# Rotary embedding without rotation products: ScalarE exchanges 32-row blocks of q and k

## The chip, the core and the metric

The program runs on one core of a Trainium2 chip. The core has four compute engines that run their own instruction streams and meet by semaphores: TensorE (matrix products into PSUM, in the profile PE, its weight loads PEld), VectorE (DVE), ScalarE (ACT) and GpSimd (POOL). SyncE (SP) issues most DMAs. The metric is the device time of one execution in microseconds, the median of several runs.

## What is computed

A transformer block of one kind (dilated attention, a rwkv recurrence, gates, a feed-forward part) is followed by one of another kind (three attention branches, memory attention, a feed-forward part), on 256 tokens of width 1024. The change touches the rotary embedding of q and k, which both blocks have in the same form:

```python
def rope(x, pos):
    half = HEAD_DIM // 2                                   # 32
    inv_freq = ROPE_THETA ** (-jnp.arange(0, HEAD_DIM, 2, dtype=jnp.float32) / HEAD_DIM)
    ang = pos[:, None] * inv_freq[None, :]
    ...
    c, s = jnp.cos(ang), jnp.sin(ang)
    x1, x2 = xf[..., :half], xf[..., half:]
    return jnp.concatenate([x1 * c - x2 * s, x2 * c + x1 * s], axis=-1).astype(x.dtype)
```

With features on partitions, a head has 64 rows. Each row needs itself times the cosine and the row 32 away, in the same head, times the sine with a sign.

## The kernel before

Everything is fp32. A large product is made of three products in a rounded format: ScalarE copies a weight tile to its rounded part (L1827, `parts<-low`), VectorE subtracts that from the tile (L2710), and TensorE multiplies both parts (L807, L808 and L816 in a chunk of features; L721 to L723 in a token range). The tile is split in two halves, 4 of its 8 rows of 128 features each in a chunk; TensorE waits for each half before its first use. Two buffers hold rounded parts, so tile j + 1 is split while TensorE works on tile j, and only after tile j - 1 is done.

Every engine's program is written out in the same order: generators for the main work and for side work are stepped by `Turns`, and each engine executes its own stream strictly in order. A moved or added instruction therefore delays all that stands behind it on its engine.

**Block one** (the profile's 92 to 152 us): `qkv()` has six chunks of q and k with 256 features and 256 tokens each (`feature_chunk`, streams of 24 products for each half of the features), and between their steps the chain of the rwkv part (`chain()`), one level a chunk, levels 1 to 5. In a level TensorE makes the T products (L1192, L1195) right at the end of a chunk, VectorE masks them out of PSUM in four instructions of 64 rows (L3002: two for the first half of the tokens, then two for the second), and TensorE makes the X products (L1217 to L1225, the first and then the second half), which wait for the masks of their half. A chunk n of q or k goes through these hands: ScalarE copies the bank to `rz1` (L1827, `mid<-psum`), VectorE multiplies the bank by the cosine (L2816), which frees the bank, TensorE multiplies `rz1` by a signed permutation into another bank (L766, at the sixth product pair of chunk n + 1), VectorE multiplies that by the sine (L2783) and adds (L2822). On VectorE the order in a chunk's turn is: cosine, masks of the level, masks of another rwkv product, sine, sum, the two split halves.

**Block two** (502 to 529 us): `main_b()` has four chunks (n = 2 to 5) of 256 features, one (n = 6) of 128, and then a token range of 464 columns. ScalarE copies the bank to `rz2`, which frees the bank; POOL multiplies by the cosine (L3701), TensorE makes the rotation (L766) inside chunk n + 1, VectorE multiplies it by the sine (L2783) from PSUM into `RC`, and POOL adds (L3706). On VectorE the order in a chunk's turn is: sine of the chunk before, then the two split halves for the next chunk. On ScalarE it is: read of the chunk that ended, then the two halves.

Of the kernel before, what the change touches and what calls it, by code (L numbers as in the profile page):

```python
# [11 lines left out]
ALU = mybir.AluOpType  # L12
# [7 lines left out]
S0 = math.exp(-0.5)  # L20


C_ID, C_SU, C_IU, C_LI, C_ONE, C_BLK, C_ROT, C_M0, C_D64 = [128 * i for i in range(9)]
C_LV = 128 * 9
C_MA = C_LV + 768
C_CA = C_MA + 768
C_ST = C_CA + 256
# [17 lines left out]
def shape_constants():  # L45
    c = np.zeros((128, C_END), np.float32)
    i = np.arange(128)
    r, s = i[:, None], i[None, :]
    c[:, C_ID:C_ID + 128] = r == s
    c[:, C_SU:C_SU + 128] = r < s  # L50
    c[:, C_IU:C_IU + 128] = r <= s
    c[:, C_LI:C_LI + 128] = r >= s
    c[:, C_ONE:C_ONE + 128] = 1
    c[:, C_BLK:C_BLK + 128] = r // 64 == s // 64
    same = r // 64 == s // 64
    c[:, C_ROT:C_ROT + 128] = (same & (r % 64 < 32) & (s % 64 == r % 64 + 32)) * 1.0 \
        - (same & (r % 64 >= 32) & (s % 64 == r % 64 - 32)) * 1.0
    for n in range(7):
        b = 1 << n
        m = (r // (2 * b) == s // (2 * b)) & (r // b % 2 == 1) & (s // b % 2 == 0)  # L60
        if n == 0:
            c[:, C_M0:C_M0 + 64] = (r % 2 == 1) & (s[:, 0:64] == r % 64 - 1)
            c[:, C_M0 + 64:C_M0 + 128] = ((r % 2 == 0) & (s[:, 0:64] == r % 64 + 1)) | (s[:, 0:64] == r % 64)
        else:
            c[:, C_LV + 128 * (n - 1):C_LV + 128 * n] = m | (r == s)
    c[:, C_D64:C_D64 + 64] = r % 64 < s[:, 0:64]
    c[:, C_D64 + 64:C_D64 + 128] = r % 64 == s[:, 0:64]
    for n, keep in enumerate([s >= r, s <= r, (r - s) % 4 == 0, ((r - s) % 4 == 0) & (s <= r),
                              (r - s) % 16 == 0, ((r - s) % 16 == 0) & (s <= r)]):
# [12 lines left out]
    c[:, C_COS:C_COS + 256] = np.tile(cos, (4, 1))  # L82
    c[:, C_SIN:C_SIN + 256] = np.tile(sin, (4, 1))
    c[0:64, C_COSC:C_COSC + 256] = np.tile(cos, (2, 1))
    c[64:128, C_COSC:C_COSC + 256] = 1
    c[0:64, C_SINC:C_SINC + 256] = np.tile(sin, (2, 1))
    return c


# [187 lines left out]
def program(nc, A, consts, vecs, pt, out):  # L277
    with ExitStack() as ctx:
# [55 lines left out]
        def const(off, n):  # L334
            return low[:, OC + off:OC + off + n]
# [234 lines left out]
        z_act, z_dve, z_pool = count("z_act"), count("z_dve"), count("z_pool")  # L570
        split_act, split_dve = count("split_act"), count("split_dve")
        main_pe, main_act, main_dve, main_pool = [count("main_" + n) for n in ("pe", "act", "dve", "pool")]
        rope_pe, rope_act, rope_dve, rope_pool = [count("rope_" + n) for n in ("pe", "act", "dve", "pool")]
        rw_pe, rw_act, rw_dve, rw_pool = [count("rwkv_" + n) for n in ("pe", "act", "dve", "pool")]
        at_pe, at_act, at_dve = [count("attn_" + n) for n in ("pe", "act", "dve")]
        up_pe, up_act, up_dve = [count("up_" + n) for n in ("pe", "act", "dve")]
# [131 lines left out]
        def tensor_program(e, turns):  # L708
# [42 lines left out]
            def seam(tag, i, at_once=False):  # L751
                yield
                if at_once:
                    for _ in turn(tag, i, XN):
                        pass
                    yield
                    yield
                else:
                    yield from turn(tag, i, XN)

            def rotate(tag, n, m, z):

                b = 2 + n % 2 if tag == "qk" else 5 + n % 3
                p = bank(b)
                q.wait_ge(*rope_act.at(tag, n))
                mm(p[:, 0:256 * m], const(C_ROT, 128), z, True, True).then_inc(rope_pe.up(tag, n), 1)  # L766
                free[b] = [rope_dve.at(tag, n)]

            def head(tag, banks, freed, late):

# [227 lines left out]
            def qkv():  # L998
                for s in range(3, 7):
                    yield from feature_chunk(st1, s, next(pg), plan_z[s][1], z_read(s), nothing)  # L1000
                yield from token_range(st1, V_AT, 2, 512, lambda i: [main_act.at("v", 0, i)], nothing)
                yield from token_range(st1, V_AT + 2, 1, 256, lambda i: [main_act.at("v", 1, i)], nothing)
                for n in range(6):
                    yield from feature_chunk(st1, QK_AT + n, next(pg), [128, 128], [rope_dve.at("qk", n, "cos")],
                                             (lambda n=n: rotate("qk", n - 1, 2, rz1[(n - 1) % 2])) if n else nothing)

            def gate(r, late):
                yield from token_range(st1, GATE_AT[r], 2, 512, lambda i: [main_act.at("g1", r, i)], late)

            def gates():  # L1010
                for r in (2, 3, 0, 1):
                    yield from gate(r, (lambda: rotate("qk", 5, 2, rz1[1])) if r == 2 else nothing)

            rw_bank = itertools.cycle((4, 5, 6, 7))

# [440 lines left out]

            st2 = ST["st2"]

            def rotate2(n):
                if n >= 2:  # L1460
                    m = 1 if n == 6 else 2
                    rotate("in2", n, m, rz2[n % 2][:, 0:m, :])

            def read2(n):
                return [main_act.at("qa", n) if n < 2 else rope_act.at("in2", n)]

            turns.beside(head("in2", (0, 2), read2, lambda n: rotate2(n - 1)), seam("in2", 1, True), 3)

            def main_b():
                for n in range(2, 7):  # L1470
                    yield from feature_chunk(st2, n - 2, next(pg), plan_2[n][1], read2(n), lambda n=n: rotate2(n - 1))
                yield from token_range(st2, 5, 2, 464, lambda i: [main_act.at("vt2", i), main_dve.at("vt2", i)], lambda: rotate2(6))

            turns.alone(main_b())

# [338 lines left out]
        def scalar_program(e, turns):  # L1814
# [3 lines left out]
            def bank(b):  # L1818
                return PSUM[:, b, :]
# [6 lines left out]
            def copy(o, a):  # L1826
                return e.activation(o, a, ACT.Copy)  # L1827
# [158 lines left out]
                turns.alone(feature_chunk(st1, s, plan_z[s][1], lambda: z_read(s, b)))  # L1986


            def rope_read(tag, n, m, b, zs):
                if n >= (2 if tag == "qk" else 4):  # L1990
                    q.wait_ge(*(rope_pe.at(tag, n - 2) if tag == "qk" else rope_pool.at(tag, n - 2)))
                copy(zs, halves(bank(b))[:, 0:m, :]).then_inc(rope_act.up(tag, n), 1)

            def qkv():
                for s in range(3, 7):
# [625 lines left out]
        def vector_program(e, turns):  # L2621
# [3 lines left out]
            def bank(b):  # L2625
                return PSUM[:, b, :]
# [151 lines left out]
                tt(rview(P + 11776 + 256 * k, 256), hid[:, k, :], rview(base + 1024, 256).bitcast(F32), ALU.subtract) \  # L2778
                    .then_inc(down_dve.up(tag, "al", k), 1)

            def rotate(tag, n, m, dst, sin):
                q.wait_ge(*rope_pe.at(tag, n))
                tt(dst, halves(bank(2 + n % 2 if tag == "qk" else 5 + n % 3))[:, 0:m, :], rep(sin, m), ALU.mult).then_inc(rope_dve.up(tag, n), 1)  # L2783


            for i in range(2):
# [30 lines left out]

            def rotate1(n):
                dst = qk[:, 2 * n:2 * n + 2, :]
                rotate("qk", n, 2, dst, const(C_SIN, 256))  # L2820
                q.wait_ge(*rope_dve.at("qk", n))
                tt(dst, dst, rt1[n % 2], ALU.add).then_inc(rope_dve.up("qk", n, "sum"), 1)  # L2822

# [472 lines left out]

            def rotate2(n):
                if n >= 2:
                    rotate("in2", n, 1 if n == 6 else 2, rope_to(n), const(C_SINC if n == 6 else C_SIN, 256))

            turns.beside(head("in2", st2, nothing, lambda n: rotate2(n - 1)), seam_ple(1), 3)

# [358 lines left out]
        def gpsimd_program(e, turns):  # L3661
# [35 lines left out]
                            yield  # L3697

            def rope(tag, n, m, zs, t1, cos):
                q.wait_ge(*rope_act.at(tag, n))  # L3700
                tt(t1, zs, rep(cos, m), ALU.mult).then_inc(rope_pool.up(tag, n, "cos"), 1)  # L3701

            def rotate(tag, n, dst, t1):
# [36 lines left out]
            def gate(r, late):  # L3740
                yield from token_range(st1, GATE_AT[r], 2, late)
# [246 lines left out]
```

## Time and profile before

| what | us |
|---|---|
| runs | 911.99, 912.70, 912.81 (median 912.7) |
| the profiled execution | 912.49, its span 910.7 |
| TensorE busy | 890.3 |
| VectorE busy | 604.7 |
| ScalarE busy | 454.3 |
| GpSimd busy | 44.3 |

The granted clock of TensorE is 0.998 of full speed over the span. Busy time of TensorE includes overlaps of neighbouring products, so starts of instructions tell more than their durations. A row of a timeline shows an instruction's start and duration; what stands in brackets is the time its engine was idle before it, and who ended that.

### The profile page before, as it was taken

How to read it: one execution, taken by the hardware profiler on the slowest of the kernel's cores; microseconds unless marked ns; L12 is line 12 of the kernel's file. 1: busy time of each engine (PE TensorE's matmuls, PEld its weight loads, DVE VectorE, ACT ScalarE, POOL GpSimd, SP SyncE). 2: the span in 40 equal slices, each digit the busy share in tenths (PEclk: the TensorE clock that was granted, in tenths of full speed). 3: DMA queues.
4: the chain of work that ended last, by engine and by line, in shares of the span. 5: the costliest groups of instructions: out<-in, count | busy, mean ns of one | idle time of the engine just before them, and what ended most of it. 6: DMA issues, size and time to landing. Idle time of an engine off the chain costs nothing.

```text
span 910.7 us, 15439 instructions
## 1 busy us (share of the span) xinstructions
PE 890.3 (98%) x6574; PEld 752.5 (83%) x6574; DVE 604.7 (66%) x966; ACT 454.3 (50%) x731; POOL 44.3 (5%) x61
## 2 busy tenths in 40 slices
PE   7999999999899999999999999999999999999997
PEld 5999988787789888888889978776788788888885
DVE  4577978557766666656766477877863566666673
ACT  4775444346443444546544356484622545555561
POOL 0010000010000000000000440000000000000000
PEclk9999999999999999999999999999999999999999
DMA  9544333233578665555339574353817566665521
GB/s 341 186 139 140 97 100 110 72 95 117 206 254 278 185 185 187 189 202 203 108 130 222 137 223 145 127 186 96 276 44 208 141 188 189 192 192 192 200 95 47
DMA packets 131205, 150.78 MB, mean 166 GB/s; under 512 B 11808, under 2 KB 102176, under 8 KB 131008
## 3 DMA queue, kind: packets, MB, share of 16 engines
q1 hardware_dynamic: 129920, 145.57, 51.6%
q10 hardware_dynamic: 1216, 4.23, 1.2%
q8 instruction: 52, 0.85, 0.4%
q14 instruction: 17, 0.14, 0.0%
HBM read 148.73 MB, written 1.05 MB: 164 GB/s over the span
## 4 chain that ended last, share of the span: by engine, by line
PE 90%; DVE 4%; ACT 2%; issue 2%; DMA 1%; POOL 0%; POOLq 0%; ACTq 0%; DVEq 0%
PE psum L834 12%; PE psum L721 10%; PE psum L723 9%; PE psum L722 9%; PE psum L839 7%; PE psum L807 4%; PE psum L808 4%; PE psum L816 4%; PE psum L787 4%; PE psum L727 3%; PE psum L883 2%; PE psum L893 2%; PE psum L884 2%; PE psum L840 2%; PE psum L1724 2%
## 5 line engine op out<-in xcount | busy, mean ns | idle before, releaser
L1827 ACT ACTIVATE parts<-low 128x1024 fp32r<-128x1024 f32 (+3 forms) x252 | 254.3, 1044 | 66.3 <-PE psum L723 50.2
L2710 DVE TENSOR_TENSOR parts<-low,parts 128x1024 fp32r<-128x1024 f32 (+3 forms) x156 | 187.9, 1234 | 27.6 <-ACT parts L1827 27.4
L721 PE MATMUL psum<-parts 128*128 128x512 f32 (+2 forms) x424 | 169.4, 399 | 1.8 <-DVE parts L2710 1.0
L723 PE MATMUL psum<-parts 128*128 128x512 f32 (+2 forms) x424 | 163.5, 386 | 0.0
L722 PE MATMUL psum<-parts 128*128 128x512 f32 (+2 forms) x424 | 163.4, 385 | 0.0
L1827 ACT ACTIVATE high<-psum 128x512 f32<-128x512 f32 (+4 forms) x95 | 52.4, 562 | 162.0 <-PE psum L840 76.4
L834 PE MATMUL psum<-parts 128*128 128x512 f32 x462 | 116.8, 392 | 0.0
L834 PEld LDWEIGHTS psum<-parts 128*128 128x128 f32 x462 | 86.9, 188 | 16.9
L721 PEld LDWEIGHTS psum<-parts 128*128 128x128 f32 x424 | 79.6, 188 | 23.3 <-issue 4.0
L723 PEld LDWEIGHTS psum<-parts 128*128 128x128 f32 x424 | 79.6, 188 | 16.3
L722 PEld LDWEIGHTS psum<-parts 128*128 128x128 f32 x424 | 79.8, 188 | 14.2 <-issue 0.2
L2775 DVE TENSOR_TENSOR parts<-low,parts 128x1024 fp32r<-128x1024 f32 x54 | 66.0, 1222 | 35.3 <-ACT parts L1827 35.3
L807 PE MATMUL psum<-parts 128*128 128x256 f32 (+2 forms) x312 | 82.3, 300 | 0.0
L808 PE MATMUL psum<-parts 128*128 128x256 f32 (+2 forms) x312 | 76.8, 282 | 0.0
L839 PEld LDWEIGHTS psum<-parts 128*128 128x128 f32 x528 | 72.0, 190 | 5.1
L839 PE MATMUL psum<-parts 128*128 128x256 f32 x528 | 73.6, 282 | 0.0
L807 PEld LDWEIGHTS psum<-parts 128*128 128x128 f32 (+2 forms) x312 | 58.9, 189 | 4.1 <-issue 3.2
L808 PEld LDWEIGHTS psum<-parts 128*128 128x128 f32 (+2 forms) x312 | 59.0, 189 | 2.3 <-issue 2.2
L3206 DVE TENSOR_TENSOR mid<-psum,high 128x512 f32<-128x512 f32 x33 | 22.8, 691 | 46.2 <-ACT high L1827 46.2
L816 PE MATMUL psum<-parts 128*128 128x256 f32 (+2 forms) x312 | 43.8, 283 | 0.0
L3669 POOL TENSOR_TENSOR low<-low 128x1 f32<-128x1 f32 x20 | 11.0, 550 | 632.3 <-DVE low L2634 316.2
L816 PEld LDWEIGHTS psum<-parts 128*128 128x128 f32 (+2 forms) x312 | 40.0, 189 | 0.1
(317 smaller groups left out, 1340.0 us busy)
## 6 DMA issues: line engine op xcount, KB each, us to landing
low<-in_w_in_dram SPq DMA_DIRECT2D x40, 1024.0 KB, 5.3
low<-in_w_ffn_in_dram SPq DMA_DIRECT2D x44, 512.0 KB, 5.2
low<-in_w_ff_in_dram SPq DMA_DIRECT2D x16, 1024.0 KB, 5.9
low<-in_w_ff_out_dram SPq DMA_DIRECT2D x16, 1024.0 KB, 4.9
low<-in_w_ffn_out_dram SPq DMA_DIRECT2D x11, 1024.0 KB, 4.9
low<-in_w_out_dram SPq DMA_DIRECT2D x8, 1024.0 KB, 5.3
low<-in_w_ple_gate_dram SPq DMA_DIRECT2D x4, 1024.0 KB, 4.9
low<-consts_dram ACTq DMA_DIRECT2D x1, 2142.0 KB, 9.0
```

Of the source, the lines that this page charges most:

```text
L721: mm(o, l[0], r[0], start, False)
L722: mm(o, l[0], r[1], False, False)
L723: return mm(o, l[1], r[0], False, stop)
L787: t = mm(PSUM[0:m, banks[n], 256 * j + 128 * i:256 * j + 128 * i + 128], w3[:, k, off:off + m], uT[:, k, 128 * i:128 * i + 128], k == 0, k ...
L807: mm(o, hi[:, k, c], st.uh[:, k, :], k == 0, False)
L808: mm(o, lo_[:, k, c], st.uh[:, k, :], False, False)
L816: t = mm(o, hi[:, k, c], st.ul[:, k, :], False, k == 7)
L834: mm(p, hi[:, k, c], st.u2(k), k == 0, False)
L839: mm(p[:, 0:256], lo_[:, k, c], st.uh[:, k, :], False, False)
L1827: return e.activation(o, a, ACT.Copy)
L2710: tt(rslot3(n, nk, width)[:, r, 0:w], slot3(n, nk, width)[:, r, 0:w], st.hi3(j)[:, r, 0:w].bitcast(F32), ALU.subtract) \
L2775: tt(rview(OR + 2048 * n + 1024 * (k % 2), 1024), slot(n)[:, 1024 * (k % 2):1024 * (k % 2) + 1024], rview(base, 1024).bitcast(F32), ALU.su ...
```

## The change

The permutation matrix `C_ROT` leaves the constants, and with it the eleven products L766 and their semaphore. The sine table carries the sign: minus in the first 32 rows of a head, plus in the others. ScalarE makes the exchange of 32-row blocks with four copies (`swapped`) out of the bank of the chunk.

- In block one these four copies take the place of the one copy to `rz1`; the cosine on VectorE still reads the bank and waits, as before, for ScalarE's read of it. The sine reads `rz1`.
- In block two the straight copy to `rz2` stays, for POOL's cosine, with a semaphore step of its own (`"z"`), and the four copies go straight to the place in `RC`; the sine then works in place there. The bank is free after the four copies.

```diff
-            def rotate(tag, n, m, z):
-
-                b = 2 + n % 2 if tag == "qk" else 5 + n % 3
-                p = bank(b)
-                q.wait_ge(*rope_act.at(tag, n))
-                mm(p[:, 0:256 * m], const(C_ROT, 128), z, True, True).then_inc(rope_pe.up(tag, n), 1)
-                free[b] = [rope_dve.at(tag, n)]
...
+            def swapped(dst, z):
+
+                for p in range(4):
+                    t = copy(dst[32 * p:32 * p + 32], z[32 * (p ^ 1):32 * (p ^ 1) + 32])
+                return t
+
             def rope_read(tag, n, m, b, zs):
-                if n >= (2 if tag == "qk" else 4):
-                    q.wait_ge(*(rope_pe.at(tag, n - 2) if tag == "qk" else rope_pool.at(tag, n - 2)))
-                copy(zs, halves(bank(b))[:, 0:m, :]).then_inc(rope_act.up(tag, n), 1)
+                z = halves(bank(b))[:, 0:m, :]
+                if tag == "qk":
+                    if n >= 2:
+                        q.wait_ge(*rope_dve.at(tag, n - 2))
+                    swapped(zs, z).then_inc(rope_act.up(tag, n), 1)
+                else:
+                    if n >= 4:
+                        q.wait_ge(*rope_pool.at(tag, n - 2, "cos"))
+                    copy(zs, z).then_inc(rope_act.up(tag, n, "z"), 1)
+                    swapped(rope_to(n), z).then_inc(rope_act.up(tag, n), 1)
...
-            def rotate(tag, n, m, dst, sin):
-                q.wait_ge(*rope_pe.at(tag, n))
-                tt(dst, halves(bank(2 + n % 2 if tag == "qk" else 5 + n % 3))[:, 0:m, :], rep(sin, m), ALU.mult).then_inc(rope_dve.up(tag, n), 1)
+            def rotate(tag, n, m, zs, dst, sin):
+                q.wait_ge(*rope_act.at(tag, n))
+                tt(dst, zs, rep(sin, m), ALU.mult).then_inc(rope_dve.up(tag, n), 1)
...
             def rope(tag, n, m, zs, t1, cos):
-                q.wait_ge(*rope_act.at(tag, n))
+                q.wait_ge(*rope_act.at(tag, n, "z"))
                 tt(t1, zs, rep(cos, m), ALU.mult).then_inc(rope_pool.up(tag, n, "cos"), 1)
```

On ScalarE in block two, from the third chunk's read to the copies that follow the half-sized chunk (`high<-psum` is the read of a chunk, `parts<-low` a split half), the order before is:

```order
L1827 ACTIVATE high<-psum 128x512
L1827 ACTIVATE parts<-low 128x4x128 x2
L1827 ACTIVATE high<-psum 128x512
L1827 ACTIVATE parts<-low 128x928 x2
L1827 ACTIVATE high<-psum 128x256
L1827 ACTIVATE high<-high 64x256 x3
```

and now, where L1810 is the same helper:

```order
L1810 ACTIVATE high<-psum 128x512
L1810 ACTIVATE high<-psum 32x512 x4
L1810 ACTIVATE parts<-low 128x4x128 x2
L1810 ACTIVATE high<-psum 128x512
L1810 ACTIVATE high<-psum 32x2x256 x4
L1810 ACTIVATE parts<-low 128x928 x2
L1810 ACTIVATE high<-psum 128x256
L1810 ACTIVATE high<-psum 32x256 x4
L1810 ACTIVATE high<-high 64x256 x3
```

Four copies have come between each read and the split halves that follow it.

On VectorE in block one, two turns with levels 1 and 2 of the chain (`mid<-psum,low` at L2816 is the cosine, L2783 the sine, L2822 the sum, L3002 the masks), the order before is:

```order
L2816 TENSOR_TENSOR mid<-psum,low 128x512
L3002 TENSOR_TENSOR high<-psum,low 64x512 x4
L2978 TENSOR_TENSOR high<-psum,low 128x4x128 x2
L2783 TENSOR_TENSOR mid<-psum,low 128x512
L2822 TENSOR_TENSOR mid<-mid 128x512
L2710 TENSOR_TENSOR parts<-low,parts 128x1024 x2
L2816 TENSOR_TENSOR mid<-psum,low 128x512
L3002 TENSOR_TENSOR high<-psum,low 64x512 x4
```

and now:

```order
L2812 TENSOR_TENSOR mid<-psum,low 128x512
L2998 TENSOR_TENSOR high<-psum,low 64x512 x4
L2974 TENSOR_TENSOR high<-psum,low 128x4x128 x2
L2779 TENSOR_TENSOR mid<-mid,low 128x512
L2818 TENSOR_TENSOR mid<-mid 128x512
L2706 TENSOR_TENSOR parts<-low,parts 128x1024 x2
L2812 TENSOR_TENSOR mid<-psum,low 128x512
L2998 TENSOR_TENSOR high<-psum,low 64x512 x4
```

Nothing has moved on VectorE; the sine alone has another source, SBUF in place of a bank.

## Rows read from the trace of the kernel before

**Rows 1.** The page: busy time by engine, and engines of the last chain.

```profile
PE 890.3 (98%) x6574; PEld 752.5 (83%) x6574; DVE 604.7 (66%) x966; ACT 454.3 (50%) x731; POOL 44.3 (5%) x61
...
PE 90%; DVE 4%; ACT 2%; issue 2%; DMA 1%; POOL 0%; POOLq 0%; ACTq 0%; DVEq 0%
```

**Rows 2.** View of line L766, block one: count, ns min/median/max, first and last start, shape.

```profile
L766 PE MATMUL psum<-mid,low x12: 590/590/594, 94.3 to 148.2; 128*128 128x512 f32 x12
```

**Rows 3.** Timeline of TensorE, a rotation of block two: start, us, engine, line, operation.

```profile
502.85 1.02 PE L766 MATMUL psum<-high,low 128*128 128x512 f32 x2
...
503.83 0.28 PE L808 MATMUL psum<-parts 128*128 128x256 f32 x1
```

**Rows 4.** Timeline of ScalarE, block two: reads of chunks, and two split halves.

```profile
495.86 0.60 ACT L1827 ACTIVATE high<-psum 128x512 f32<-128x512 f32 x1 [1.09 <-PE psum L787]
496.35 2.00 ACT L1827 ACTIVATE parts<-low 128x1024 fp32r<-128x1024 f32 x2
501.61 0.60 ACT L1827 ACTIVATE high<-psum 128x512 f32<-128x512 f32 x1 [3.26 <-PE psum L816]
...
521.43 0.60 ACT L1827 ACTIVATE high<-psum 128x512 f32<-128x512 f32 x1 [4.97 <-PE psum L816]
```

**Rows 5.** Timeline of VectorE, block two: a sine and the two split halves behind it.

```profile
503.91 0.69 DVE L2783 TENSOR_TENSOR high<-psum,low 128x512 f32<-128x512 f32 x1 [4.12 <-PE psum L766]
504.60 1.22 DVE L2710 TENSOR_TENSOR parts<-low,parts 128x1024 fp32r<-128x1024 f32 x1
...
505.75 2.31 DVE L2710 TENSOR_TENSOR parts<-low,parts 128x1024 fp32r<-128x1024 f32 x1
```

**Rows 6.** Timeline of GpSimd in the same stretch: a cosine and a sum.

```profile
502.29 1.28 POOL L3701 TENSOR_TENSOR high<-high,low 128x512 f32<-128x512 f32 x1 [15.90 <-ACT high L1827]
504.68 2.30 POOL L3706 TENSOR_TENSOR high<-high 128x512 f32<-128x512 f32 x1 [1.11 <-DVE high L2783]
```

**Rows 7.** Timeline of TensorE: the token range's first product, and its first after both waits.

```profile
525.51 0.47 PE L721 MATMUL psum<-parts 128*128 128x464 f32 x1 [0.39 <-DVE parts L2710]
...
527.63 0.48 PE L721 MATMUL psum<-parts 128*128 128x464 f32 x1 [0.17 <-DVE parts L2710]
```

**Rows 8.** Groups of ScalarE with shapes apart: a copy of 15 rows; busy us, mean ns.

```profile
L1827 ACT ACTIVATE high<-psum 15x512 f32<-15x512 f32 x1 | 0.6, 568 | 0.0
```

**Rows 9.** Timeline of ScalarE, block one: reads in levels 3 to 5; pairs of 64-row copies.

```profile
123.21 0.60 ACT L1827 ACTIVATE mid<-psum 128x512 f32<-128x512 f32 x1 [1.92 <-PE psum L816]
...
134.37 0.60 ACT L1827 ACTIVATE mid<-psum 128x512 f32<-128x512 f32 x1 [1.92 <-PE psum L816]
...
145.31 0.60 ACT L1827 ACTIVATE mid<-psum 128x512 f32<-128x512 f32 x1 [1.98 <-PE psum L816]
...
151.37 1.08 ACT L1827 ACTIVATE high<-psum 64x512 f32<-64x512 f32 x2 [3.57 <-PE psum L1221]
...
152.47 1.21 ACT L1827 ACTIVATE high<-psum 64x512 f32<-64x512 f32 x2
```

**Rows 10.** Timeline of VectorE, block one: start of its work, masks of level 1, level 3.

```profile
90.51 0.45 DVE L2964 COPY_PREDICATED high<-low,psum 128x256 f32<-128x256 int32 x1 [0.99 <-PE psum L1132]
...
103.47 2.84 DVE L3002 TENSOR_TENSOR high<-psum,low 64x512 f32<-64x512 f32 x4
...
123.83 0.69 DVE L2816 TENSOR_TENSOR mid<-psum,low 128x512 f32<-128x512 f32 x1 [2.80 <-ACT mid L1827]
124.44 2.84 DVE L3002 TENSOR_TENSOR high<-psum,low 64x512 f32<-64x512 f32 x4
```

**Rows 11.** Timeline of TensorE, block one: first X product of levels 1, 3, 4, 5.

```profile
106.55 0.27 PE L1217 MATMUL psum<-high 64*64 64x64 f32 x1
...
129.17 0.27 PE L1217 MATMUL psum<-high 64*64 64x64 f32 x1
...
139.73 0.27 PE L1217 MATMUL psum<-high 64*64 64x64 f32 x1
...
150.13 0.27 PE L1217 MATMUL psum<-high 64*64 64x64 f32 x1
```

More of the change, by code:

```diff
@@ L20 @@
 S0 = math.exp(-0.5)
-C_ID, C_SU, C_IU, C_LI, C_ONE, C_BLK, C_ROT, C_M0, C_D64 = [128 * i for i in range(9)]
-C_LV = 128 * 9
+C_ID, C_SU, C_IU, C_LI, C_ONE, C_BLK, C_M0, C_D64 = [128 * i for i in range(8)]
+C_LV = 128 * 8
 C_MA = C_LV + 768
@@ L54, in shape_constants @@
     c[:, C_BLK:C_BLK + 128] = r // 64 == s // 64
-    same = r // 64 == s // 64
-    c[:, C_ROT:C_ROT + 128] = (same & (r % 64 < 32) & (s % 64 == r % 64 + 32)) * 1.0 \
-        - (same & (r % 64 >= 32) & (s % 64 == r % 64 - 32)) * 1.0
     for n in range(7):
@@ L82, in shape_constants @@
     c[:, C_COS:C_COS + 256] = np.tile(cos, (4, 1))
-    c[:, C_SIN:C_SIN + 256] = np.tile(sin, (4, 1))
+    c[:, C_SIN:C_SIN + 256] = np.tile(np.concatenate([-sin, sin]), (2, 1))
     c[0:64, C_COSC:C_COSC + 256] = np.tile(cos, (2, 1))
     c[64:128, C_COSC:C_COSC + 256] = 1
-    c[0:64, C_SINC:C_SINC + 256] = np.tile(sin, (2, 1))
+    c[0:64, C_SINC:C_SINC + 256] = np.concatenate([-sin, sin])
     return c
@@ L572, in program @@
         main_pe, main_act, main_dve, main_pool = [count("main_" + n) for n in ("pe", "act", "dve", "pool")]
-        rope_pe, rope_act, rope_dve, rope_pool = [count("rope_" + n) for n in ("pe", "act", "dve", "pool")]
+        rope_act, rope_dve, rope_pool = [count("rope_" + n) for n in ("act", "dve", "pool")]
         rw_pe, rw_act, rw_dve, rw_pool = [count("rwkv_" + n) for n in ("pe", "act", "dve", "pool")]
@@ L1003, in qkv @@
                 for n in range(6):
-                    yield from feature_chunk(st1, QK_AT + n, next(pg), [128, 128], [rope_dve.at("qk", n, "cos")],
-                                             (lambda n=n: rotate("qk", n - 1, 2, rz1[(n - 1) % 2])) if n else nothing)
+                    yield from feature_chunk(st1, QK_AT + n, next(pg), [128, 128], [rope_dve.at("qk", n, "cos")], nothing)
             def gate(r, late):
@@ L1011, in gates @@
                 for r in (2, 3, 0, 1):
-                    yield from gate(r, (lambda: rotate("qk", 5, 2, rz1[1])) if r == 2 else nothing)
+                    yield from gate(r, nothing)
             rw_bank = itertools.cycle((4, 5, 6, 7))
@@ L1457, in tensor_program @@
             st2 = ST["st2"]
[L1459 to L1462, printed above, removed]
             def read2(n):
                 return [main_act.at("qa", n) if n < 2 else rope_act.at("in2", n)]
-            turns.beside(head("in2", (0, 2), read2, lambda n: rotate2(n - 1)), seam("in2", 1, True), 3)
+            turns.beside(head("in2", (0, 2), read2, nothing), seam("in2", 1, True), 3)
             def main_b():
                 for n in range(2, 7):
-                    yield from feature_chunk(st2, n - 2, next(pg), plan_2[n][1], read2(n), lambda n=n: rotate2(n - 1))
-                yield from token_range(st2, 5, 2, 464, lambda i: [main_act.at("vt2", i), main_dve.at("vt2", i)], lambda: rotate2(6))
+                    yield from feature_chunk(st2, n - 2, next(pg), plan_2[n][1], read2(n), nothing)
+                yield from token_range(st2, 5, 2, 464, lambda i: [main_act.at("vt2", i), main_dve.at("vt2", i)], nothing)
             turns.alone(main_b())
@@ L2819, in rotate1 @@
                 dst = qk[:, 2 * n:2 * n + 2, :]
-                rotate("qk", n, 2, dst, const(C_SIN, 256))
+                rotate("qk", n, 2, rz1[n % 2], dst, const(C_SIN, 256))
                 q.wait_ge(*rope_dve.at("qk", n))
@@ L3298, in rotate2 @@
                 if n >= 2:
-                    rotate("in2", n, 1 if n == 6 else 2, rope_to(n), const(C_SINC if n == 6 else C_SIN, 256))
+                    rotate("in2", n, 1 if n == 6 else 2, rope_to(n), rope_to(n), const(C_SINC if n == 6 else C_SIN, 256))
             turns.beside(head("in2", st2, nothing, lambda n: rotate2(n - 1)), seam_ple(1), 3)
```

## Prediction

> **What bounds the kernel now.** The page first: TensorE is busy 890.3 of 910.7 us, and 90% of the chain that ended last is TensorE's own work [rows 1]. So a product taken off TensorE is worth its whole time, as long as nobody whom TensorE waits for gets later. Then the view of the line that goes: its twelve records in block one are six products, since one fp32 product runs as two records [rows 2]. TensorE's timeline prices one: the rotation begins at 502.85 and the second chunk product behind it at 503.83, while chunk products follow each other every 0.12 us; 0.98 - 0.12 leaves 0.86 a rotation [rows 3]. ScalarE's reads, which begin as a chunk ends, say the same: 5.75 us for the chunk without a rotation (495.86 to 501.61), and 19.82 for the next three (to 521.43), 6.61 each [rows 4]. Ten rotations of 512 columns and one of 256: 10 x 0.86 + 0.43 = **9.0 us** leaves TensorE.
>
> **What is added.** ScalarE reads a q or k chunk with four copies of 32 rows (block one, in place of one copy), or with the straight copy and then four (block two). No row shows a 32-row copy. A copy of 15 rows and 512 columns takes 568 ns, about as long as one of 128 rows (0.60 in [rows 4]), so rows are not what is paid for [rows 8]. The open question is how densely they follow. Copies of 64 rows stand at a step of 0.49 where both read the same half of the partitions (1.08 for two) and of 0.61 where the half changes (1.21 for two) [rows 9]. The new copies change their rows each time, so I take **0.60**, with 0.49 as the lower end. ScalarE's read then takes 2.4 instead of 0.6 in block one, and 0.49 + 2.4 = 2.9 in block two. ScalarE is idle before these reads (3.26 and 4.97 us in [rows 4]), so its own time is covered; what costs is what stands behind the read on VectorE: in block one the cosine on the same bank and, behind it, the masks of the rwkv chain; in block two the sine and both halves of the weight split. The sine itself gets no dearer from SBUF: a split half with both inputs there takes 1.22 for 1024 columns, the sine from the bank 0.69 for 512 [rows 5]. The constants' transfer, 3% shorter, ends long before these places: nothing.
>
> **Block one, by levels of the chain.** Times count from s, the start of ScalarE's read. Before, the cosine begins at s + 0.62 (123.21, 123.83), the four masks L3002 at s + 1.23, the first pair ends at s + 2.65 and the second at s + 4.07 [rows 9, 10]. After, all of it is 1.8 later (2.4 for 0.6): pairs at 4.45 and 5.87, with 0.1 for the semaphore **4.55 and 5.97**. TensorE comes to the first half of the X products (L1217) at s + 5.96, 5.36 and 4.82 in levels 3, 4 and 5 (129.17, 139.73, 150.13) [rows 9, 11]; level 2 lies as level 3. Without the rotation that stands ahead of them it comes 0.86 sooner, and to the second half 1.0 later than to the first.
> - Level 1: two rotations are gone, and TensorE would come at 104.8 instead of 106.55. But VectorE has worked from 90.5 on, and its masks end at 104.9 and 106.31 [rows 10]; the second half begins at 106.4 instead of 107.5. Gain 1.1 of 1.7.
> - Levels 2 and 3: 5.10 against 4.55 needed, 6.10 against 5.97. No wait; gain 2 x 0.86.
> - Level 4: 4.50 and then 5.55, against 4.55 and 5.97: waits 0.45. Gain 0.4.
> - Level 5: 3.96 against 4.55, then 5.55 against 5.97: waits 1.0. Gain -0.1.
>
> Block one: 1.1 + 1.7 + 0.4 - 0.1 = **3.1 us** of 5.2. The splits of the next weights end 1.8 later too, but TensorE comes to them only after the next level's first products, over 1 us behind them.
>
> **Block two.** Here the splits decide. Before, POOL's sum starts right behind the sine, and then POOL and VectorE hinder each other: the sum takes 2.30 where the cosine of the same size takes 1.28, and a split half takes 2.31 where the one before it took 1.22 [rows 5, 6]. I read this as turns: VectorE's half (to 505.75), the sum (to 507.0), VectorE's other half (to 508.05). After: copies until s + 2.9, sine until 3.6, and now the sum is first, because ScalarE's half comes only at 3.85 (two halves take 2.00 [rows 4]); sum until 5.0, VectorE's halves done at **6.15 and 7.3**. TensorE, without its rotation, ends the chunk at 5.75 and wants the second half 0.96 (eight products) after the first: at the third chunk it waits 0.4 + 0.2. By that delay it finds the halves ready one chunk on, and the ones after have 512 columns. Three rotations less the wait: 3 x 0.86 - 0.6 = 2.0.
>
> The last place costs. Behind the fourth chunk (read at 521.43) stands a half-sized chunk of 2.9 us, and then the token range, whose weights can be split only after that read. Before, the range begins at 525.51, waiting for VectorE, and its second part at 527.63, which is 6.24 after the fourth chunk's end (0.04 before the read); between them lie six products, 2.12 less the rotation's 0.43 and the wait's 0.17, 1.5 [rows 4, 7]. After: copies 2.9, sine 3.6, sum 5.0, a half of 928 columns to 6.05; the range begins at s + 6.1 and its second part at s + 7.6. That is **1.4 later**, though two rotations stood here. Block two is worth 2.0 - 1.4 = **0.6**.
>
> The Trainium skill, page "SBUF — State Buffer", section "Who interferes with whom", says that a VectorE instruction with two SBUF inputs and a GpSimd one that reads SBUF exclude each other for a whole instruction; the sine gets its first input from SBUF now and would join them. By that rule, the rows on split and sum agree (2.31 against 1.22). It would speak against this change only where the sine meets POOL's cosine; that is over 2.0 after s (502.29 + 1.28 against 501.61 [rows 4, 6]) and the sine begins at s + 2.95, so the sum stays as it is.
>
> **Sum.** 3.1 + 0.6 = **3.7 us** saved. The profiled execution took 912.49 us (span 910.7 and 1.8 around it), the median of the runs is 912.7: **909.0**.
>
> **Rivals.**
> - *Dense copies.* At a step of 0.49 block one's read is done at 2.0, so that levels 4 and 5 wait 0.1 and 0.7 (3.8 saved); in block two the third chunk doesn't wait and the range's second part is 0.9 late: 2.6 - 0.9 = 1.7. Together 5.5, **907.2**. For it: pairs on the same rows show 0.49. Against: the pair that changes rows shows 0.61. Chance 0.20.
> - *All of it hidden.* 9.0 saved, **903.7**. Against: in level 1 VectorE is busy for 16 us before its masks, whatever TensorE does. 0.06.
> - *Absorbed later.* Behind 155 us gates, attention and rwkv share an order fixed in advance. If another engine bounds a stretch there, block one's gain is lost and block two's 0.6 is left: **912.1**, no change. For it: TensorE is idle for 20.4 us of the span. Against: 90% of the chain is TensorE, so most of what it waits for was released by itself and moves along. 0.14.
> - *Slower: the 32-row copies are dearer than every row here.* The same places: at a step of 0.9 the masks are 1.2 later still, the levels wait 0.4, 1.0, 1.0, 1.5 and 2.0, and block one loses 0.7; in block two the third chunk waits 1.8 and the range's second part is 2.5 late: 2.6 - 1.8 - 2.5 = -1.7. Together -2.4, **915.1**. It is no gain from a step of 0.78, and slower beyond doubt from 0.88. Against: copies of 15, 64 and 128 rows all take 0.57 to 0.61. 0.07.
>
> **How the numbers follow.** The forecast has 0.53. About 0.2%, 1.8 us, can be told from no change by a measurement of this kernel. Faster: forecast, dense and hidden, 0.79; same: 0.14; slower: 0.07. The range reaches from 905.8, below the dense copies, to 911.6; it leaves out all hidden, slower and half of absorbed.
>
> **What would show it.** In the profile after: eleven products fewer; 32-row copies of 0.59 at a step of 0.60; block one's cosine 2.4 behind ScalarE's read; new waits of TensorE for the masks in levels 1, 4 and 5, none in 2 and 3; in block two a short wait for the split at the third chunk and one of about 3 us before the token range, with POOL's sum back at 1.3 and ahead of the split. A step under 0.5 or over 0.7, or a range that begins without a long wait, would make the sum wrong; so would new idle time behind 155 us.

## The result and the profile after

| what | before | after |
|---|---|---|
| median of the runs, us | 912.81 (911.99 to 912.85, five runs) | 915.81 (915.40 to 917.31, five runs) |
| the profiled execution, us | 912.49, span 910.7 | 915.76, span 914.0 |
| TensorE busy, us | 890.3 | 884.0 |
| ScalarE busy, us | 454.3 | 476.8 |

The changed kernel takes 1.0041 times as long (95% interval 1.0029 to 1.0052): its median is **3.0 us higher**, where 3.7 us less was forecast, and lies above the range of 905.8 to 911.6.

The page of the kernel after, its busy times and the shares of the last chain, answers to [rows 1]:

```profile
PE 884.0 (97%) x6552; PEld 750.7 (82%) x6552; DVE 604.7 (66%) x966; ACT 476.8 (52%) x769; POOL 41.3 (5%) x61
...
PE 85%; DVE 8%; ACT 4%; issue 2%; DMA 1%; POOL 0%; POOLq 0%; ACTq 0%; DVEq 0%
```

The 22 records of the eleven rotations are gone. But VectorE and ScalarE, which had 6% of the chain, now have 12%: the chain leaves TensorE more often. The question is where.

**Block one.** The timeline of ScalarE after gives the reads of levels 2 to 5, now four copies in a row each (start, duration of the four, in brackets the idle time ahead):

```profile
111.97 2.38 ACT L1810 ACTIVATE mid<-psum 32x512 f32<-32x512 f32 x4 [1.98 <-PE psum L805]
123.56 2.39 ACT L1810 ACTIVATE mid<-psum 32x512 f32<-32x512 f32 x4 [1.98 <-PE psum L805]
135.15 2.39 ACT L1810 ACTIVATE mid<-psum 32x512 f32<-32x512 f32 x4 [1.98 <-PE psum L805]
147.25 2.38 ACT L1810 ACTIVATE mid<-psum 32x512 f32<-32x512 f32 x4 [1.98 <-PE psum L805]
```

Four copies take 2.39, a step of 0.60 as forecast. But from 123.56 to 135.15 it is 11.59, where it was 11.16 before [rows 9], although a rotation has gone from each chunk. TensorE's timeline after names who it waits for, at the first X product of each half in levels 3, 4 and 5, and of the first half in level 1 (L1205 was L1217; level 2 reads as level 3):

```profile
106.39 0.24 PE L1205 MATMUL psum<-high 64*64 64x64 f32 x1 [1.27 <-DVE high L2998]
...
129.57 0.24 PE L1205 MATMUL psum<-high 64*64 64x64 f32 x1 [0.82 <-DVE high L2998]
...
130.89 0.24 PE L1205 MATMUL psum<-mid,high 64*64 64x64 f32 x1 [0.16 <-DVE high L2981]
...
141.16 0.24 PE L1205 MATMUL psum<-high 64*64 64x64 f32 x1 [1.42 <-DVE high L2998]
...
142.98 0.24 PE L1205 MATMUL psum<-mid,high 64*64 64x64 f32 x1 [0.65 <-DVE mid L2988]
...
151.82 0.24 PE L1205 MATMUL psum<-high 64*64 64x64 f32 x1 [0.57 <-DVE high L2998]
...
153.26 0.24 PE L1205 MATMUL psum<-mid,high 64*64 64x64 f32 x1 [0.28 <-DVE high L2998]
```

And this is the view of waits from 85 to 160 us (us in total, times, the longest):

```profile
DVE mid L2812 <- ACT mid L1810: 12.8, 4, 3.2
...
PE psum L1205 <- DVE high L2998: 5.2, 6, 1.4
```

VectorE's cosine (L2812) waits for the read, and TensorE waits 5.2 us for the masks behind it (L2998), also in levels 2 and 3, for which no wait was forecast. In VectorE's timelines, the first of the custom instructions that follow the chain, of the kernel before and of the kernel after, shows that the place is left 2.20 us later:

```profile
154.70 0.56 DVE L3090 CUSTOM_DVE_ANT_1 mid<-psum,low 128x384 f32<-128x384 f32 x1 [1.60 <-PE psum L1346]
```

```profile
156.90 0.56 DVE L3086 CUSTOM_DVE_ANT_1 mid<-psum,low 128x384 f32<-128x384 f32 x1
```

**From there to block two** nothing changes. The first read of [rows 4] that a rotation follows, at 501.61, now stands at 503.84, 2.23 later.

**Block two.** ScalarE's timeline after has the reads 5.75, 6.74 and 5.76 apart, 18.25 for three chunks, where it was 19.82:

```profile
503.84 3.02 ACT L1810 ACTIVATE high<-psum 128x512 f32<-128x512 f32 x5 [3.26 <-PE psum L805]
...
509.59 3.01 ACT L1810 ACTIVATE high<-psum 128x512 f32<-128x512 f32 x5 [0.70 <-PE psum L805]
...
516.33 3.02 ACT L1810 ACTIVATE high<-psum 128x512 f32<-128x512 f32 x5 [1.69 <-PE psum L805]
...
522.09 3.02 ACT L1810 ACTIVATE high<-psum 128x512 f32<-128x512 f32 x5 [1.56 <-PE psum L805]
```

GpSimd's sum takes 1.29 and not 2.30 [rows 6], and VectorE's two split halves behind it end at 507.98 + 3.20 = 511.18, 7.34 behind the read:

```profile
507.66 1.29 POOL L3702 TENSOR_TENSOR high<-high 128x512 f32<-128x512 f32 x1 [1.86 <-DVE high L2779]
```

```profile
507.98 3.20 DVE L2706 TENSOR_TENSOR parts<-low,parts 128x1024 fp32r<-128x1024 f32 x2 [0.40 <-ACT parts L1810]
```

Then the token range, in TensorE's timeline after. It begins 6.22 behind the fourth read, after the only long wait of the stage, and the sixth product stands 0.38 behind the fifth where 0.21 is the usual step:

```profile
528.31 0.45 PE L718 MATMUL psum<-parts 128*128 128x464 f32 x1 [3.38 <-DVE parts L2706]
...
529.01 0.40 PE L718 MATMUL psum<-parts 128*128 128x464 f32 x1
529.22 0.58 PE L719 MATMUL psum<-parts 128*128 128x464 f32 x1
529.60 0.59 PE L720 MATMUL psum<-parts 128*128 128x464 f32 x1
```

The view by stretches of time says what that is. The columns are: the stretch, its length, busy time and count of PE, PEld, DVE, ACT and POOL, the granted clock of TensorE, the busy share of the DMA engines, GB/s:

```profile
524.80:528.20 3.40, 0.13 (x2) 0.00 (x0) 2.75 (x3) 3.30 (x7) 2.00 (x2) 1.00 1.02 225
528.20:529.20 1.00, 0.89 (x4) 0.86 (x5) 1.00 (x1) 0.96 (x3) 0.56 (x1) 1.00 1.00 381
529.20:532.40 3.20, 3.20 (x10) 2.59 (x10) 1.97 (x4) 2.86 (x5) 2.25 (x3) 0.50 1.03 403
532.40:536.00 3.60, 3.60 (x18) 3.22 (x17) 1.11 (x2) 0.75 (x1) 3.60 (x15) 0.97 0.14 56
```

A microsecond after the wait the granted clock is 0.50, the lower of its two levels (1.2 GHz), for 3.2 us. In the kernel before it is 1.00 at this place, with the DMA engines just as busy:

```profile
528.00:530.00 2.00, 2.00 (x11) 1.80 (x10) 1.03 (x1) 1.81 (x2) 1.86 (x4) 1.00 1.06 401
```

The two waits of [rows 7] had been 0.39 and 0.17.

As a marker of the end of this stage serves the read of twelve columns on ScalarE, at 534.53 before and 538.00 after. It has moved by 3.47 us, of which 2.23 came from block one; block two adds 1.24.

### The profile page after: what moved, and what is told of

Read it like the earlier page. It is cut to its first block, busy times and chain, and to the rows that moved or that the text cites. A ratio compares the mean times of both kernels' runs of the same rounds, so it can differ in the third digit from the quotient of the medians.

```text
span 914.0 us, 15434 instructions
## 1 busy us (share of the span) xinstructions
PE 884.0 (97%) x6552; PEld 750.7 (82%) x6552; DVE 604.7 (66%) x966; ACT 476.8 (52%) x769; POOL 41.3 (5%) x61
## 4 chain that ended last, share of the span: by engine, by line
PE 85%; DVE 8%; ACT 4%; issue 2%; DMA 1%; POOL 0%; POOLq 0%; ACTq 0%; DVEq 0%
PE psum L823 12%; PE psum L718 9%; PE psum L720 9%; PE psum L719 9%; PE psum L828 7%; PE psum L776 4%; PE psum L796 3%; PE psum L797 3%; PE psum L805 3%; PE psum L724 3%; PE psum L872 2%; PE psum L882 2%; PE psum L873 2%; PE psum L829 2%; PE psum L1707 2%
## 5 line engine op out<-in xcount | busy, mean ns | idle before, releaser
L1810 ACT ACTIVATE parts<-low 128x1024 fp32r<-128x1024 f32 (+3 forms) x252 | 254.3, 1044 | 66.4 <-PE psum L720 51.4
L1810 ACT ACTIVATE high<-psum 128x512 f32<-128x512 f32 (+6 forms) x115 | 63.3, 559 | 143.3 <-PE psum L829 76.4
L796 PE MATMUL psum<-parts 128*128 128x256 f32 (+2 forms) x312 | 79.1, 291 | 0.9 <-ACT high L1810 0.6
L797 PE MATMUL psum<-parts 128*128 128x256 f32 (+2 forms) x312 | 76.5, 283 | 0.0
L1810 ACT ACTIVATE mid<-psum 32x512 f32<-32x512 f32 (+7 forms) x55 | 29.2, 547 | 31.9 <-PE psum L805 13.5
L805 PE MATMUL psum<-parts 128*128 128x256 f32 (+2 forms) x312 | 43.8, 283 | 0.0
```

What stands on the lines that cost most here:

```text
L796: mm(o, hi[:, k, c], st.uh[:, k, :], k == 0, False)
L797: mm(o, lo_[:, k, c], st.uh[:, k, :], False, False)
L805: t = mm(o, hi[:, k, c], st.ul[:, k, :], False, k == 7)
```

## Experiments

A run's marks are read at three places: the read that ends a chunk at each level, the instruction with which block one is left (154.70 before, 156.90 after), and the twelve-column read (534.53 and 538.00). A is in each expectation the theory that is being put forward, B its rival.

**Where it is lost: each block alone.** The first kernel has the change in block one only, with block two's rotation restored:

```diff
-                    copy(zs, z).then_inc(rope_act.up(tag, n, "z"), 1)
-                    swapped(rope_to(n), z).then_inc(rope_act.up(tag, n), 1)
+                    copy(zs, z).then_inc(rope_act.up(tag, n), 1)
...
+                    yield from feature_chunk(st2, n - 2, next(pg), plan_2[n][1], read2(n), lambda n=n: rotate2(n - 1))
```

> Block one alone as in the changed kernel, block two with its rotation products and single copies as before. Theory A (the first half of a level's X products waits for all four masks, because its two PSUM banks are the ones that the masks read, and the second half waits for the next two masks for the same reason): each level loses what is measured in the trace of the changed kernel, 2.2 us by the end of block one, so 915.0. Rival B (block one follows the prediction, 3.1 us saved, and block two loses all): 909.7. Rival C (both blocks lose half): 914.4.

Measured: 914.81 against 912.75 of the kernel before on the same chip, 1.0026 (1.0015 to 1.0037). The second is the other half, with block one's read again a single copy and its rotations restored:

> Block two alone as in the changed kernel, block one as before. Theory A (block two loses 1.3 us: a wait of 3.4 us before the token range, after which TensorE runs at half its clock for some 3 us): 914.1, with the same wait and the same slow stretch. Rival B (block two loses nearly all of the 3 us): 915.8. Rival C (block two keeps the predicted 0.6 when block one doesn't shift it): 912.2.

Measured: 913.56 (911.89 to 914.82) against 912.75, 1.0009 (1.0000 to 1.0018). Its 3.38 us wait and the fall of the clock are there, in the timeline of TensorE and in the view by stretches:

```profile
526.06 0.72 PE L719 MATMUL psum<-parts 128*128 128x464 f32 x1 [3.38 <-DVE parts L2716]
```

```profile
526.00:529.00 3.00, 2.94 (x8) 2.59 (x9) 1.82 (x2) 2.88 (x7) 1.61 (x3) 0.52 1.04 410
```

So +2.1 and +0.8 make up +2.9 of the whole +3.0. Block one is a loss by itself; block two hardly differs from no change in the median, though its marks are 0.95 later.

**What the X products wait for.** The code has an answer that I had passed over. Four banks go round in a cycle for the rwkv products. In levels 1 to 4, the T products take two, another product takes the next two, the first half of the X products takes the two of T again, and the second half those of the other product. What frees the two banks of T is written under the T products:

```python
                        for g in range(2):
                            free[bs[g]] = [rw_dve.at("T", i, lv, g) for i in range(2)]
```

Both halves of the tokens have to be masked, all four masks, and the second half of X waits for two masks that stand behind those (L2974 or L2981, at level 4 the copies L2988). In level 5 there is no other product between T and X, so the first half takes two banks that ScalarE has long read; there it stands 4.57 behind ScalarE's read (151.82, 147.25) and the second half 6.01 (153.26), which is the need that the prediction had worked out. This kernel gives the other product the banks 2 and 3 for the first half of the tokens, so that X no longer follows T in the same banks:

```diff
+                def own(i):
+                    return (2, 3) if i == 0 else [next(rw_bank) for _ in range(2)]
...
-                    bs = [next(rw_bank) for _ in range(2)]
+                    bs = own(i)
```

> The changed kernel, but the products that are masked by the third mask pair (received, keyed, below for the first half of the tokens) use banks 2 and 3, which the rotation left, and the chain cycles through banks 4 to 7 alone; so the banks of the first half of X are free one level earlier and those of the second half with the four masks. Theory A (banks make the wait): X waits as the prediction worked out, first half at 4.55 and second at 5.97 us after ScalarE's read begins; block one saves 3.1 instead of losing 2.2, and the time is 915.8 - 5.3 = 910.5. Rival B (the data of the masks, or ScalarE's copies themselves, make the wait): no change, 915.8.

Measured: 912.01 against 912.75, 0.9994 (0.9985 to 1.0003), 3.8 us less than the changed kernel. The rows are those of ScalarE's timeline (levels 2 to 5), of TensorE's, of the view of waits from 85 to 160 us, and of VectorE's exit:

```profile
110.68 2.39 ACT L1813 ACTIVATE mid<-psum 32x512 f32<-32x512 f32 x4 [1.97 <-PE psum L805]
121.34 2.39 ACT L1813 ACTIVATE mid<-psum 32x512 f32<-32x512 f32 x4 [1.96 <-PE psum L805]
132.14 2.39 ACT L1813 ACTIVATE mid<-psum 32x512 f32<-32x512 f32 x4 [2.04 <-PE psum L805]
142.94 2.39 ACT L1813 ACTIVATE mid<-psum 32x512 f32<-32x512 f32 x4 [1.98 <-PE psum L805]
```

```profile
115.79 0.27 PE L1208 MATMUL psum<-high 64*64 64x64 f32 x1
```

```profile
PE psum L1208 <- DVE high L3004: 1.3, 4, 0.6
```

```profile
152.59 0.56 DVE L3092 CUSTOM_DVE_ANT_1 mid<-psum,low 128x384 f32<-128x384 f32 x1
```

The copies take as long as in the changed kernel and the data are ready as late; only the banks are others. In level 2 the first X product comes 5.11 behind the read instead of 6.0, without a wait, and block one is left 4.3 us earlier. Bank reuse is shown as the cause of block one's loss. The expectation had 5.3 for these 4.3, and 910.5 for the whole, 1.5 less than measured.

**Whether the slow read alone does it.** Here all rotations are kept, and block one's read is cut in four straight copies of 32 rows:

```diff
+                    for p in range(4):
+                        t = copy(zs[32 * p:32 * p + 32], z[32 * p:32 * p + 32])
+                    t.then_inc(rope_act.up(tag, n), 1)
```

> The kernel before with its rotation products, but block one's read of a q or k chunk is made of four 32-row copies in place (no exchange), so that only the lateness of the cosine and of the masks is added, 1.8 us, and nothing is taken off TensorE. Theory A (need at 5.97 and 7.2 us after the read, levels arrive at 5.96, 5.96, 5.36, 4.82): waits of 0.2 in levels 2 and 3, 1.4 in level 4 and 1.2 in level 5, together 3.0: 915.8. Rival B (need at 4.55 and 5.97): 0.2 in level 5, 913.0.

Measured: 916.32 against 912.75, 1.0041 (1.0028 to 1.0053). ScalarE's timeline, levels 2 to 4:

```profile
113.47 2.39 ACT L1825 ACTIVATE mid<-psum 32x512 f32<-32x512 f32 x4 [1.98 <-PE psum L814]
125.06 2.39 ACT L1825 ACTIVATE mid<-psum 32x512 f32<-32x512 f32 x4 [1.98 <-PE psum L814]
136.66 2.39 ACT L1825 ACTIVATE mid<-psum 32x512 f32<-32x512 f32 x4 [1.98 <-PE psum L814]
```

The step of a level is 11.59 to 11.60 here as well, with a rotation in it. So in the middle levels it is set by read, cosine, four masks and the X products, and TensorE's 0.86 has no place in it: taken away or not, the level lasts 11.59. The time is 0.5 us over what A expected. TensorE waits 1.14 us for ScalarE at the first rotation (L764, at 95.56), which the expectation did not have. That the rows do not change halves in these copies and still take 2.39 also shows that the exchange costs nothing over a straight copy of 32 rows.

**Cosine first.** If the masks are what counts, VectorE need not wait for ScalarE. From the third chunk on, the cosine waits for TensorE only, and ScalarE's copies wait for the cosine:

```diff
+                        q.wait_ge(*rope_dve.at(tag, n, "cos"))
...
-                q.wait_ge(*rope_act.at("qk", n))
+                q.wait_ge(*(rope_act.at("qk", n) if n < 2 else main_pe.at("st1", QK_AT + n, 1)))
```

> The changed kernel, but from the third q or k chunk of block one on VectorE's cosine waits for the chunk's product alone and ScalarE's four copies wait for the cosine; the bank is free after the copies. Theory A (what block one loses is the lateness of cosine and masks behind ScalarE's 2.4 us): masks are done as early as before or 0.6 earlier, TensorE doesn't wait in levels 2 to 5 and keeps 4 x 0.86, and 0.1 in level 1: block one goes from 2.2 lost to 3.5 saved, 915.8 - 5.7 = 910.1. Rival B (the load on ScalarE itself, its splits 0.7 us later still, makes the wait): 915.8 or more.

Measured: 912.11 against 912.45, 0.9999 (0.9990 to 1.0008): 0.3 below the kernel before, where the changed kernel is 3.0 above its own runs of it and A had expected 2.7 below. Of TensorE's waits for the masks from 85 to 160 us, that of level 1 is left and 0.2 at each of two other places. Block one is left at 152.21, 4.7 earlier than in the changed kernel (A: 5.7) and 2.5 earlier than before:

```profile
PE psum L1205 <- DVE high L2999: 1.3, 1, 1.3
```

```profile
152.21 0.56 DVE L3087 CUSTOM_DVE_ANT_1 mid<-psum,low 128x384 f32<-128x384 f32 x1 [0.87 <-PE psum L1334]
```

**What the clock costs in block two.** Three fp32 products of 512 columns that nothing reads are put ahead of the token range, so that TensorE is idle for 0.79 us there instead of 3.38:

```diff
+                p = bank(5)
+                for _ in range(3):
+                    mm(p, const(C_ONE, 128), const(C_LV, 512), True, True)
```

> The changed kernel with three fp32 products of 512 columns (0.86 us each, into a bank that nobody reads) put on TensorE ahead of block two's token range, into its wait of 3.4 us. Nothing else differs. Theory A (TensorE's clock falls to half because it stood idle, and the fall costs nine products 0.17 us each): granted clock 1.00 in the whole stretch, 1.5 us less, 914.3. Rival B (the fall has another cause, for instance the DMA load of 400 GB/s at that place, or it costs nothing since VectorE is late anyway): same clock or same time, 915.8.

Measured: 914.82 against 912.45, 1.0028 (1.0018 to 1.0037). TensorE's timeline, and the stretch in which the clock had been 0.50:

```profile
524.93 2.74 PE L1457 MATMUL psum<-low 128*128 128x512 f32 x6
528.46 0.45 PE L718 MATMUL psum<-parts 128*128 128x464 f32 x1 [0.79 <-DVE parts L2709]
```

```profile
528.00:532.00 4.00, 3.54 (x16) 2.90 (x17) 2.76 (x4) 3.87 (x8) 2.60 (x4) 1.00 1.01 366
```

The token range begins at the same time (0.15 later, as the whole block does), and the twelve-column read comes at 536.84 instead of 538.00: with the block's later entry (504.01 for 503.84) that is 1.33 us given back by useless work. The DMA engines move as much there as before (366 GB/s), and the clock is 1.00, so their load is not what lowers it. In the profiled executions the fall of the clock costs 1.3 us at this mark. The medians show less, and less surely: 2.4 above the kernel before instead of 3.0, with runs from 913.88 to 916.77.

**Splits first in block two.** ScalarE makes the straight copy, then its split halves, and only then the exchange, out of SBUF; the sine moves behind VectorE's halves:

```diff
                     copy(zs, z).then_inc(rope_act.up(tag, n, "z"), 1)
-                    swapped(rope_to(n), z).then_inc(rope_act.up(tag, n), 1)
+
+            def exchange(n):
+                if n >= 2:
+                    q.wait_ge(*rope_act.at("in2", n, "z"))
+                    swapped(rope_to(n), rz2[n % 2][:, 0:1 if n == 6 else 2, :]).then_inc(rope_act.up("in2", n), 1)
```

> The changed kernel, but in block two ScalarE makes the straight copy (which frees the bank), then the two split halves, and only then the four exchange copies, out of SBUF; VectorE makes its sine behind its split halves; the keys' copies move behind the split of the token range's second slot. Theory A (block two is lost by what stands behind the exchange copies, the splits): no wait of TensorE for the splits except 0.2 us, all 3.9 us of rotations saved, no idle time long enough to lower the clock: 915.8 - 1.3 - 3.7 = 910.8. Rival B (q and k are ready 2.7 us later than before, and the branches that read them wait): half or all of it is given back, 912.5 to 915.

Measured: 912.55 against 912.45, 1.0003 (0.9995 to 1.0012): 0.1 above the kernel before, 2.9 less than the 3.0 of the changed kernel; 5.0 less had been expected. TensorE's and ScalarE's timelines:

```profile
525.15 0.45 PE L718 MATMUL psum<-parts 128*128 128x464 f32 x1 [0.70 <-DVE parts L2717]
...
536.16 0.47 PE L718 MATMUL psum<-parts 128*128 128x512 f32 x1 [0.65 <-ACT low L1806]
```

```profile
506.47 2.01 ACT L1810 ACTIVATE parts<-low 128x1024 fp32r<-128x1024 f32 x2 [1.89 <-DMA low<-in_w_in_dram]
```

The long wait and the fall of the clock are gone, and the twelve-column read stands at 534.43. What is missing from the expected gain lies in three places. At the first chunk ScalarE waits 1.89 for the weights' transfer, a wait that the changed kernel does not have behind its copies; this makes the next splits late, and TensorE's product at 516.53 comes some 0.35 late. Before the token range TensorE waits 0.70 where 0.2 was expected. And behind the range it waits 0.65; the view names ScalarE's small read, which now stands behind the exchange.

**Both orders together, and the banks.** The last two are the two reorderings in one kernel, and the same with the six banks:

> Both: cosine first from the third chunk of block one, splits first in block two. Theory A: the gains add, 912.8 - 3.5 - 3.7 = 905.6. Rival B (one is absorbed by the other or by the stretch between): 908 to 911.

Measured: 908.72 against 912.45, 0.9958 (0.9945 to 0.9970), 3.7 less than the kernel before. A's 905.6 was added up from gains that had only been forecast, and the time lies in B's range; but B's mechanism does not show. By their medians the two orders had given 3.3 and 2.9 against the changed kernel, 6.2 together, and the kernel with both gives 6.7. Its block one, the same code as in the cosine-first kernel, is left at 153.34 instead of 152.21, without a wait for another engine that the other lacks; the view of waits has 0.5 us of "issue" in the X products there and 0.8 plus 0.3 here, which is about half the difference of 1.13. The rest stays open.

> Both orders (cosine first, splits first) and the banks 2 and 3 for the third pair of masks. What is left of waits in block one with both orders is 1.3 us in level 1, where the first half of the X products waits for the banks of all four masks. Theory A (banks): that wait goes, 908.7 - 1.3 = 907.4. Rival B (the wait is for the masks' data, or is paid back in level 2): 908.7.

Measured: 907.20 against 912.44, 0.9946 (0.9932 to 0.9959), where A expected 907.4. The wait of level 1 is gone too, block one is left at 151.66, 3.04 us earlier than before, and this is the fastest kernel here, 5.2 us below the one before.

## Why the prediction was wrong

**Right: what a rotation is worth, and what a copy costs.** Block two's first chunk takes 5.75 instead of 6.61, 0.86 less. The copies have the step of 0.60 (the five of block two take 3.02, for 2.9 worked out), so the rival with dense copies is out, and so is the slower one, whose 915.1 rests on a mechanism (a step of 0.9) that isn't there. The cosine begins 2.42 behind the read, as worked out.

**Wrong: the need of the X products, "first half at 4.55, second at 5.97".** This is the step that failed. It let each half of the X products wait for the masks of its own half, and the description of the kernel ahead of it says so too. Before, TensorE came to them after all four masks, so no wait showed what they need. With the bank cycle, the first half needs all four masks, forecast for 5.87 behind the read and with 0.1 for the semaphore 5.97: the trace after has 6.00, 6.01 and 6.01 (117.97 behind 111.97, 129.57 behind 123.56, 141.16 behind 135.15). The second half needs the two masks behind them and comes at 7.3 (130.89). The durations of the step were right; the event was not, in levels 1 to 4. In level 5, where the banks do not bind, the forecast holds (4.57 and 6.01), and with six banks it holds in level 4 too (136.72 and 138.16 behind 132.14: 4.58 and 6.02). By level, gains taken from the reads and the exit:

| from | to | forecast | after | with six banks |
|---|---|---|---|---|
| start | read of level 2 | 1.1 | 0.1 | 1.4 |
| read of level 2 | of level 3 | 0.86 | -0.4 | 0.5 |
| of level 3 | of level 4 | 0.86 | -0.4 | 0.4 |
| of level 4 | of level 5 | 0.4 | -1.2 | 0.1 |
| of level 5 | exit | -0.1 | -0.3 | -0.3 |
| sum | | 3.1 | -2.2 | 2.1 |

The last column shows what is left of the error when that step is mended by hand: 1.0 us. The 1.3 us of waits in that kernel do not explain it, since 1.1 of them are in levels 4 and 5, where waits of 0.45 and 1.0 had been forecast. What does not fit are the X products themselves in levels 2 and 3: from the first one to the next chunk's product they take 2.38 (115.79 to 118.17) and 2.52 us (126.45 to 128.97), where it was 2.02 before (129.17 to 131.19 in level 3), without a wait for another engine. Why stays open.

**Right in kind, too small: the third chunk of block two.** Forecast a wait of 0.6, found 6.74 - 5.75 = 1.0; VectorE's halves end 7.34 behind the read, for 7.3 forecast, with the sum ahead of them at 1.29. The first half ends at 510.05, 6.21 behind the read for 6.15 forecast, and the third chunk begins at 510.19. The sum had TensorE ready at 5.75 behind the read, but a chunk's first product stands 0.20 ahead of the read (503.64, 503.84), so it was ready at 5.55. The trace puts 0.63 of the wait down to ScalarE's read at 509.59; the code makes the chunk wait only for its bank, free since 506.86, and for the split, so I take the split as the cause. Three chunks gained 1.57 instead of 2.0.

**Right and then missed: the token range.** It begins 6.22 behind the fourth read, for 6.1. What the sum left out is that the wait of 3.4 us would take the clock down behind it. From the fourth read to the twelve-column read it was 13.10 before and is 15.91: 2.8 later and not 1.4, and the filled wait gave 1.3 of that back. The Trainium skill, page "TensorE: Matmul & The Clock Gate", section "HAM oscillation — how this bites in real kernels", tells of an engine that is throttled across a wait and starts its next stretch at the lower clock. The kernel with block two alone agrees: from the second product behind the wait on, the products stand 0.38 to 0.39 apart, at a granted clock of 0.52 from 526 to 529. The changed kernel agrees in kind only: the first microsecond behind the wait is still at 1.00, and 0.50 follows from 529.2 to 532.4. I had the wait in the sum and should have asked what the clock does behind it.

**Right: nothing is absorbed later.** The delay of 2.20 at the exit of block one is 2.23 at block two. The rival of no change had reckoned with a gain being swallowed; here a loss was carried whole.

In sum: forecast -3.7, found +3.3 in the profiled executions. Of the 7.0 between them 5.3 are block one's: 4.3 came back with the six banks, so they are the bank cycle's, and the cause of 1.0 stays open. 1.4 are the token range's, nearly all of it the clock, and 0.4 the third chunk's; 0.2 came back behind the marks. The slower rival's 915.1 came near the measured 915.8 by luck.

## What to carry to other kernels

Before an edit delays a read of PSUM, list for each product behind it not only whose data it takes but whose bank it takes over, and which instruction frees that bank: an event that never showed as a wait is not in the profile, only in the code. Where copies get longer, put the reader on whose heels the critical engine stands first, and let the longer one follow; the two reorderings here turned a loss of 3.0 us into a gain of 3.7, and own banks into 5.2. A wait of several microseconds on TensorE has to be priced with what the clock does after it.

## What the runs showed of the hardware

**Rows don't count, nor which rows.** A copy of 32 rows and 512 columns takes 0.59 on ScalarE, at a step of 0.60 whether its rows change places (2.39 for four) or not (2.39). From SBUF, four take 2.55 (splits first, 508.51). Why pairs of 64 rows stand 0.49 apart in [rows 9] and these 0.60, no run shows.

**The clock can fall without a long wait.** The profiled execution of the kernel with block one alone took 916.26, its median is 914.81. The view by stretches shows the reason, first this execution, then the changed kernel at the same place with the same waits of 1.42 and 0.65:

```profile
140.00:142.00 2.00, 0.73 (x49) 0.76 (x53) 1.91 (x4) 0.00 (x0) 0.00 (x0) 1.00 0.00 0
142.00:144.00 2.00, 1.34 (x64) 1.24 (x58) 1.87 (x5) 1.09 (x2) 0.00 (x0) 0.75 0.00 0
144.00:146.00 2.00, 2.00 (x45) 1.88 (x40) 2.00 (x3) 0.89 (x2) 0.00 (x0) 0.50 0.03 8
```

```profile
140.00:142.00 2.00, 0.83 (x56) 0.87 (x60) 1.88 (x5) 0.00 (x0) 0.00 (x0) 1.00 0.00 0
142.00:144.00 2.00, 1.35 (x87) 1.24 (x78) 1.90 (x4) 1.09 (x2) 0.00 (x0) 1.00 0.00 0
144.00:146.00 2.00, 2.00 (x27) 1.93 (x18) 2.00 (x3) 1.09 (x2) 0.00 (x0) 1.00 0.04 8
```

Behind the same two waits of about a microsecond, with small products between them, the clock was at 0.50 in one execution and at 1.00 in the other; level 4 lasted 13.52 instead of 12.10. It is likely to be part of why runs of the kernels with such waits spread by 2 us; only this one execution shows it.

**GpSimd and VectorE hinder each other also where I had not counted on it.** In the changed kernel GpSimd's cosine of the second chunk begins at 510.27, while VectorE's split half runs until 511.18. It takes 2.06 instead of 1.29, and no wait of TensorE comes of it:

```profile
510.27 2.06 POOL L3697 TENSOR_TENSOR high<-high,low 128x512 f32<-128x512 f32 x1 [1.31 <-ACT high L1810]
```
